# Mixture-of-experts encoder layer on one core: order of an expert's last steps, and the shape of a transpose

## The reference

```python
cap = max(1, EC_FACTOR * n // N_EXPERTS)          # 64 prompt tokens, 128 sample tokens
aff = jax.nn.softmax((hf @ w_router).astype(jnp.float32), axis=-1)
g, idx = lax.top_k(aff.T, cap)
xe = hf[idx]
hid = jax.nn.silu(jnp.einsum('ecd,edf->ecf', xe, w_gate)) * jnp.einsum('ecd,edf->ecf', xe, w_up)
ye = jnp.einsum('ecf,efd->ecd', hid, w_down) * g[..., None].astype(h.dtype)
y = jnp.zeros((n, D), h.dtype).at[idx.reshape(-1)].add(ye.reshape(-1, D))
```

## Time and profile before

| | us |
|---|---|
| median of 3 runs | 3680.63 |
| lowest, highest | 3666.42, 3682.62 |
| profiled execution | 3670.78 |
| its span, first to last instruction | 3669.0 |
| TensorE matmuls busy | 3365.4 (92%) |
| VectorE busy | 2361.5 (64%) |
| ScalarE busy | 1933.4 (53%) |

### The profile page before, as it was taken

One profiled execution on the slowest core, in us unless ns is written; L12 is line 12 of the kernel. 1 busy time (PEld: TensorE's weight loads), 2 busy tenths in 40 slices (PEclk: granted clock), 3 DMA queues, 4 the chain that ended last, 5 costly groups with the idle time before them and its releaser, 6 DMA issues. The chain is left out here.

```text
span 3669.0 us, 50589 instructions
## 1 busy us (share of the span) xinstructions
PE 3365.4 (92%) x18510; PEld 2903.6 (79%) x18510; DVE 2361.5 (64%) x3652; ACT 1933.4 (53%) x3202; POOL 151.3 (4%) x213
## 2 busy tenths in 40 slices
PE   8598886999819999999999999999999999999998
PEld 1386654557708998999999999899989989999997
DVE  0278872674375767676776766676676766766675
ACT  0623332555505666566565665565565556565564
POOL 0000000000000001000010100010000100000000
PEclk9699988999959999999999999999999999999999
DMA  8401113505235566575765747566565756657562
GB/s 320 125 26 49 49 48 125 176 32 191 98 138 190 211 248 234 194 271 195 259 224 220 255 173 268 213 241 234 208 247 190 275 211 236 237 189 264 201 247 89
DMA packets 143922, 697.39 MB, mean 190 GB/s; under 512 B 12452, under 2 KB 39588, under 8 KB 120164
## 3 DMA queue, kind: packets, MB, share of 16 engines
q1 hardware_dynamic: 132196, 659.75, 48.4%
q0 software_dynamic: 7392, 25.96, 3.1%
q10 hardware_dynamic: 4132, 8.65, 0.7%
HBM read 656.51 MB, written 37.80 MB: 189 GB/s over the span
## 5 line engine op out<-in xcount | busy, mean ns | idle before, releaser
L1197 PE MATMUL psG<-xe,w_gu_hi_part 128*128 128x384 f32 x5632 | 1650.9, 364 | 30.9 <-DVE w_gu_lo_part L1387 25.2
L1199 PE MATMUL psG<-xe,w_gu_lo_part 128*128 128x192 f32 x5632 | 1418.3, 252 | 0.0
L1197 PEld LDWEIGHTS psG<-xe,w_gu_hi_part 128*128 128x128 f32 x5632 | 1064.1, 189 | 52.7 <-DVE w_gu_lo_part L1387 30.6
L1199 PEld LDWEIGHTS psG<-xe,w_gu_lo_part 128*128 128x128 f32 x5632 | 1085.2, 193 | 7.0
L1387 DVE TENSOR_TENSOR w_gu_lo_part<-raw_gu,w_gu_hi_part 128x1024 fp32r<-128x1024 f32 x704 | 859.8, 1223 | 117.7 <-ACT w_gu_hi_part L1301 117.6
L1301 ACT ACTIVATE w_gu_hi_part<-raw_gu 128x1024 fp32r<-128x1024 f32 x704 | 741.5, 1056 | 12.8 <-DMA raw_gu<-in_w_gu 12.8
L1421 DVE TENSOR_TENSOR gu<-psG,low 128x384 f32<-128x384 f32 x352 | 196.1, 557 | 647.0 <-ACT low L1330 647.0
L1392 DVE TENSOR_TENSOR w_dn_lo_part<-raw_dn,w_dn_hi_part 128x1024 fp32r<-128x1024 f32 x352 | 431.3, 1225 | 9.7 <-ACT w_dn_hi_part L1311 9.6
L1330 ACT ACTIVATE low<-psG 128x384 f32<-128x384 f32 x352 | 172.3, 490 | 456.9 <-PE psG L1199 456.6
L1311 ACT ACTIVATE w_dn_hi_part<-raw_dn 128x1024 fp32r<-128x1024 f32 x352 | 367.9, 1045 | 0.0
L1290 ACT ACTIVATE xst<-psG,modv,a 128x128 f32<-128x128 f32 (+1 forms) x272 | 102.2, 427 | 462.9 <-PE psG L1199 395.8
(11 more groups left out here) (156 smaller groups left out, 3464.1 us busy)
## 6 DMA issues: line engine op xcount, KB each, us to landing
raw_gu<-in_w_gu SPq DMA_DIRECT2D x176, 2048.0 KB, 7.9
raw_dn<-in_w_down SPq DMA_DIRECT2D x176, 1024.0 KB, 8.9
aw<-in_ada_w SPq DMA_DIRECT2D x12, 2048.0 KB, 8.9
bias<-in_bias SPq DMA_DIRECT2D x8, 1536.0 KB, 11.1
w_raw<-in_w_in SPq DMA_DIRECT2D x20, 512.0 KB, 5.3
qk_d<-zg SPq DMA_DIRECT2D x8, 768.0 KB, 3.6
qk<-qk_d SPq DMA_DIRECT2D x8, 768.0 KB, 10.7
out<-wo_raw SPq DMA_DIRECT2D x12, 512.0 KB, 2.6
```

The lines of the kernel that those rows point to most:

```text
L1197: pe.matmul(bank[:, 0:2 * CAP], wh, xe[:, k, :, :].rearrange("p a b -> p (a b)"), start=(k == 0), stop=False, skip_group_check=True)
L1199: mm = pe.matmul(bank[:, 0:CAP], wl, xe[:, k, 0, :], start=False, stop=(k == KD - 1), skip_group_check=True)
```

## The change

- The last two gate/up steps of an expert run back to back, and the last four downs (18 to 21) behind them.
- In step 21 the token split moves ahead on both engines: on ScalarE behind `low`, ahead of silu; on VectorE behind the sum, ahead of the product. ScalarE's `hi_down(21)` moves ahead of its wait for the product.
- The down weights get three slots instead of two, hs four instead of three; `hi_down` waits for the last user of its slot.
- xg_p gets 128 rows. Rows 64 to 127 are zeroed once by GpSimd, and the prompt tokens are turned as a 128x128 tile; ScalarE still reads 64 columns of the result.
- The last expert is written out on TensorE as its own copy and turns nothing; the loop has experts 1 to 14. GpSimd gathers nothing in the last expert.

```diff
-    HS = 3
+    HS, DS = 4, 3
...
-        d_hi = sb(c, "w_dn_hi_part", [P, 2, D], F32R)
-        d_lo = sb(c, "w_dn_lo_part", [P, 2, D], F32R)
+        d_hi = sb(c, "w_dn_hi_part", [P, DS, D], F32R)
+        d_lo = sb(c, "w_dn_lo_part", [P, DS, D], F32R)
...
-        xg_p = sb(c, "xg_p", [CAP_P, D])
+        xg_p = sb(c, "xg_p", [P, D])
...
-                    pe.transpose(psG[:, bank + 1, 2 * CAP:2 * CAP + CAP_P], xg_p[:, :].rearrange("p (d k) -> p k d", k=KD)[:, k, :],
-                                 ident[0:CAP_P, 0:CAP_P]).then_inc(x_turned, 1)
+                    pe.transpose(psG[:, bank + 1, 2 * CAP:2 * CAP + P], xg_p[:, :].rearrange("p (d k) -> p k d", k=KD)[:, k, :],
+                                 ident[:, :]).then_inc(x_turned, 1)
...
+                pe.wait_ge(xp_rest, 1)
...
-                    if turned_in(i) is not None:
+                    if turned_in(i) is not None and not last:
...
-                        wh, wl = (w[:, a, h * 512:(h + 1) * 512] for w in (d_hi, d_lo))
+                        wh, wl = (w[:, i % DS, h * 512:(h + 1) * 512] for w in (d_hi, d_lo))
...
-                def expert(e, first):
-                    for i in range(FT + BEHIND):
-                        if i < FT:
-                            gate_up(e, i, first)
+                def expert(e, first, last):
+                    for i in range(FT - 2):
+                        gate_up(e, i, first, last)
                         if i >= BEHIND:
                             down(e, i - BEHIND, first)
-                expert(0, True)
-                with pe.Fori(1, EXPERTS) as e:
-                    expert(e, False)
+
+                    gate_up(e, FT - 2, first, last)
+                    gate_up(e, FT - 1, first, last)
+                    for i in range(FT - 2 - BEHIND, FT):
+                        down(e, i, first)
+                expert(0, True, False)
+                with pe.Fori(1, EXPERTS - 1) as e:
+                    expert(e, False, False)
+                expert(EXPERTS - 1, False, True)
...
+                pool.memset(xg_p[CAP_P:P, :], 0.0).then_inc(xp_rest, 1)
+                pool.wait_ge(xp_rest, 1)
...
-                    if not (first and i < 2):
-                        act.wait_ge(dn_done, e * FT + i - 1)
-                    act.activation(d_hi[:, i % 2], raw_dn[:, s, i % 2], ACT.Copy).then_inc(dn_hi, 1)
+                    back = last_user(i, DS, FT)
+                    if not (first and back < 0):
+                        act.wait_ge(dn_done, e * FT + back + 1)
+                    act.activation(d_hi[:, i % DS], raw_dn[:, s, i % 2], ACT.Copy).then_inc(dn_hi, 1)
...
                     act.activation(low[:, a], psG[:, 2 * a:2 * a + 2, CAP:2 * CAP], ACT.Copy).then_inc(gu_low, 1)
                     if nxt and i < FT - 1:
                         hi(*nxt, 0)
+                    if nxt and i == FT - 1:
+                        xsplit(e + 1)
                     act.wait_ge(gu_sum, n + 1)
                     act.activation(sl[:, a, :], gu[:, a, 0, :], ACT.Silu).then_inc(silu_done, 1)
                     if nxt and i < FT - 1:
                         hi(*nxt, 1)
+                    if i == FT - 1:
+                        hi_down(e, i, first)
...
-                    hi_down(e, i, first)
+                    if i < FT - 1:
+                        hi_down(e, i, first)
                     if nxt and i == FT - 1:
-                        xsplit(e + 1)
                         hi(*nxt, 0)
                         hi(*nxt, 1)
...
                     if nxt and i < FT - 1:
                         lo(*nxt, 0)
+                    if nxt and i == FT - 1:
+                        xsplit(e + 1)
                     dve.wait_ge(gu_sum, n + 1)
                     dve.wait_ge(silu_done, n + 1)
```

## The result

The changed kernel takes 3620.63 us in the median of four runs (3617.45 to 3624.79), against 3677.62 us for the kernel before, timed with it. The ratio is 0.984, with a 95% interval of 0.9823 to 0.9856: 57 us or 1.6% less. The profiled execution took 3617.6 us with a span of 3615.8; the one of before had a span of 3669.0.

The account below looks back on a forecast made before the run. TensorE's own instruction stream was taken to bound the expert stage, with holes at expert changes, turns and clock dips. 39.6 + 1 + 4.6 + 8.8 + 2.5 + 0.8 + 10 = 67.3 us off 3670.8 gives 3604 us, range 3580 to 3630.

Parts of the forecast that it names:

- The turn: Transposing prompt tokens, 15 experts: two full tiles take 0.22 us instead of 0.63 or 0.52; 39.6 us saved.
- Rival A: Transposing prompt tokens: the full tile gives nothing, the 0.24 us hole belongs to transposing; 3644 us, chance 0.14.
- The last expert: Last expert on TensorE: its eight turns of the next tokens go; 4.6 us saved.
- The jump's start: Change of expert: low down weights end 6.5 us after the last gate/up, before 4.85, so the jump starts 1.65 us later.
- T: Time mark at each change of expert: the end of the expert's last gate/up (1421.11 us before).
- The jumps: 13 loop jumps left at changes of expert: 0.68 us saved each, a hole of 1.8 us stays; 8.8 us.
- B: Change of expert: the whole jump hides behind queued downs, 23 us more saved; 3581 us, chance 0.10.
- D: Change of expert: the down weights' low part becomes the bound; slower, for instance 3718 us, chance 0.02.
- Rival C: Change of expert: the hole stays (split engines or code fetch slower), the dips with it; 3623 us, chance 0.16.
- The exit and the ends: Change from expert 14 to 15 leaves the loop, 2.5 us; first change and last expert lose the dn_lo wait, 0.8 us.
- The clock's dips: After changes of expert: TensorE idle falls from 2.05 to about 1.37 us, so six clock dips go; 10 us saved.
- The eight turns ahead of the first expert: Before the expert loop: turns paced by ScalarE, 0 to 2 us saved, 1 us taken.

Follow-up runs that it names:

- tile-alone run: Kernel before with only the full 128x128 tile for the prompt tokens, old order, slots and loop; 3635.5 us against 3678.3, ratio 0.9888.
- the changed kernel with the shift: Changed kernel with 12 increments of an unused semaphore ahead of TensorE's loop, nothing else; 3615.8 us, ratio to before 0.9835.
- rotated loop with the shift: Changed kernel with TensorE's loop jump ahead of down 21 and 12 increments of an unused semaphore ahead of the loop; 3646.7 us.
- rotated loop: Changed kernel with TensorE's loop jump moved ahead of down 21, order of instructions kept; 3704.3 us, ratio to before 1.0069.

## Why the prediction was right, point by point

The forecast of 3604 us was low by 17 us, inside its range of 3580 to 3630. By its steps:

- **The turn** (39.6 us): right in mechanism and size. A turn costs 0.23 us (0.22 forecast) for all k, so 15 x (4.60 - 8 x 0.23) = 41.4 us; the slower pitch for k below 4, of which I had kept half, is gone. The tile alone gave 43 us with the last expert included. Rival A falls.
- **The last expert** (4.6 us): its eight turns are gone from the profile.
- **The jump's start** (T+6.5 for the low weights): measured T+6.54, the jump at T+6.7.
- **The jumps** (8.8 us): 13 x (11.71 - 10.86) = 11.1 us. They took 3.76 us in the mean this time and 3.96 before; that is the difference, and it is luck: with the order of steps as before, in the tile-alone run, they took 3.78 us, and in the changed kernel with the shift 3.96. B falls by the hole that stays, D by the low weights' time.
- **Rival C** (3623 us) has the time nearest to the measured 3620.6, but not by its mechanism: the hole did not stay at 2.5 us (1.76), and the low weights were on time. Only a part of its dips came.
- **The exit and the ends** (2.5 and 0.8 us): the exit 9.45 + 2.33 - 9.10 = 2.7 us; the first change and the last expert 0.54 us each.
- **The clock's dips** (10 us): this step failed. It put the idle time at a jump at 1.37 us in the mean, below four changes idle for 1.42 to 1.98 us that brought no dip, and expected none. Its own window of 11.03 us less the 9.25 us of four downs gives 1.78 us, inside that range. Measured, the idle time is 10.86 - 9.27 = 1.59 us in the mean and 1.1 to 2.0 us at the single changes. Dips came after four of them, idle for 1.95, 1.71, 1.95 and 1.85 us (the 1.71 at 2042.99:2053.96), while 2.01 us at another change (11.27 us) brought none. So "no dip after up to 1.98 us" was a rule made from four cases. Over the seven profiles with a hole at each jump the experts had 6 (before), 4 (after), 2, 1, 1, 2 and 5 dips, and none in the three kernels without a loop. By length: none of the 48 holes under 1.7 us idle was followed by a dip, 11 of the 27 between 1.7 and 2.0 us were, 10 of the 18 longer ones, and all 13 in the rotated loop with the shift, idle for 2.1 to 3.1 us. A longer hole makes a dip likelier; what decides for one of 1.7 to 2.5 us these runs do not show. The dips cost 6.6 us instead of 10.0, so this is worth 3.4 us here.
- **The eight turns ahead of the first expert** (1 us): from the first of them to the first gate/up 10.07 us instead of 10.47. Behind that the first three gate/ups took 16.47 instead of 15.95 us, at a granted clock of 0.82 instead of 0.86. Together nothing.

From the first gate/up on these sum to 41.4 + 4.6 + 11.1 + 2.7 + 1.1 + 3.4 - 0.5 = 63.8 us, against 63.1 us between the two profiles and 66.3 forecast. The other miss lies in none of the edits. I made the sum against the profiled execution and called it quick, but did not carry that into the forecast: its stages ahead of the experts were 9.8 us earlier than those of the profile after. In the medians 57.0 us are left of the 67.3.

The reading behind it held better than the sum. The waits list of before named VectorE's w_gu_lo_part for the hole, and both the change's early token split and its reordering fit that name; the jump's line and the 7.31 us of the change without one said otherwise, and the runs without the loop bear them out: they keep every wait, and no hole is left. What I had not drawn from it is that the early split works against the change: I had priced it (T+6.5 against T+4.85) without asking what the other order would give.

## What to carry to other kernels

Where a big loop body runs on TensorE, look at the line of the loop's jump before believing who a wait at the loop's edge is put down to; the jump cost up to 4.3 us here, could be hidden only in part, and writing the experts out (3589 us) was worth more than reordering around it. Keep the row height of neighbouring weight loads equal: padding a 64-row transpose to 128 rows took a turn from up to 0.63 to 0.23 us, with twice the rows. And judge a gain of ten microseconds in a kernel with stages at a varying clock stage by stage, for the rest of the program moved by as much.

## What the hardware showed that I had not expected

- A taken jump on TensorE is not cheaper for starting early. Started at T+6.7 it lasted 3.76 us in the mean, at T+5.8 4.20 us, at T+2.9, with four microseconds of downs still queued, 6.6 us in the median. The instructions' packet came 1.0 us after the jump's start in the median in the first case and 4.2 us after it in the last; why is open. ScalarE's and VectorE's jumps of the same loop take 0.05 us.
- In the rotated loop a second stop followed three matmuls behind the jump's target, 54.3 us at 13 jumps, with one more 16 KB packet of instructions per jump (181 instead of 168). Both were taken away by 12 idle instructions ahead of the loop.
- A change of the weights' height from 128 to 64 rows or back cost 0.24 us one way and some 0.16 us the other (0.27 us between two loads instead of 0.11); a second load of the same height came 0.10 us behind the first.
- Twenty-one of 93 holes at a jump were followed by a dip of the clock of 1.6 to 1.8 us, none of the 48 that were shorter than 1.7 us.
- Nearly the same code ahead of the experts began the first gate/up anywhere from 1114.4 to 1130.6 us in twelve profiles, by the clock granted there.
